# Another placement of the modulation products and five small reorderings in a hand-scheduled fp32 kernel of two transformer blocks

## The reference

```python
for l in range(DEPTH):                                  # DEPTH = 2
    mod_x = (s_x @ w_mod[l] + b_mod[l])[:, None, :]     # (1024) @ (1024, 6144)
    mod_c = s_c @ w_mod[l] + b_mod[l]
    sh1_x, sc1_x, g1_x, sh2_x, sc2_x, g2_x = jnp.split(mod_x, 6, axis=-1)
    h_x = modulate(rms_norm(x, norm_g[l, 0]), sh1_x, sc1_x)
    h_c = modulate(rms_norm(ctx, norm_g[l, 0]), sh1_c, sc1_c)
    m_x, m_c = even_mixer(...) if l == 0 else odd_mixer(...)
    x = x + g1_x * rms_norm(m_x, norm_g[l, 1])
    f_x = squared_relu_mlp(modulate(rms_norm(x, norm_g[l, 2]), sh2_x, sc2_x), w_mlp_in[l], w_mlp_out[l])
    x = x + g2_x * rms_norm(f_x, norm_g[l, 3])
    # the same for ctx in layer 0
```

## Time and profile before

| | us |
|---|---|
| three runs | 1677.31, 1679.67, 1682.97 (median 1679.67) |
| the profiled execution | 1677.31 |
| its span, first to last instruction | 1675.5 |
| mean granted clock of TensorE | 0.968 of full speed |

### The profile page before, as it was taken

How to read it: one execution, slowest core, us unless ns; L and a number is a source line. 1 busy time by engine, 2 the same in 40 slices (tenths; PEclk the granted TensorE clock), 3 DMA queues, 4 the chain that set the end, 5 groups by cost and what they waited for, 6 DMA issues and landing times.

```text
span 1675.5 us, 24174 instructions
## 1 busy us (share of the span) xinstructions
PE 1536.0 (92%) x9546; PEld 1307.6 (78%) x9546; DVE 904.1 (54%) x1513; ACT 677.0 (40%) x1095; POOL 157.7 (9%) x121
## 2 busy tenths in 40 slices
PE   7999899999999568998898999999998988869997
PEld 7998698998987455785688777777787776768886
DVE  6776744544546684436764433333457645555444
ACT  4553444444444324425554222222234534444442
POOL 3100400000000300000014001111002020021110
PEclk9999999999999788999999999999999999979999
DMA  6456555344436123411111543543413510224451
GB/s 247 160 201 227 207 204 201 132 171 140 163 128 229 56 76 151 152 51 51 75 65 62 201 155 147 201 175 140 188 51 110 167 64 1 109 112 176 182 200 52
DMA packets 43338, 233.75 MB, mean 140 GB/s; under 512 B 13088, under 2 KB 14048, under 8 KB 16352
## 3 DMA queue, kind: packets, MB, share of 16 engines
q1 hardware_dynamic: 30944, 222.38, 35.4%
q10 hardware_dynamic: 12288, 9.88, 2.1%
HBM read 231.16 MB, written 1.08 MB: 139 GB/s over the span
## 4 chain that ended last, share of the span: by engine, by line
PE 79%; DVE 11%; ACT 5%; issue 3%; POOL 1%; DMA 1%; ACTq 0%; DVEq 0%; SPq 0%; POOLq 0%
PE ps L516 22%; PE ps L517 21%; PE ps L518 21%; PE ps L719 5%; DVE wlo L979 3%; PE ps L606 2%; PE ps L658 2%; ACT whi L969 2%; PE ps L692 2%; PE ps L650 1%; PE ps L568 1%; POOL flo L2106 1%; DVE nmax L1682 1%; PE ps L590 1%; DVE nmax L1710 1%
## 5 line engine op out<-in xcount | busy, mean ns | idle before, releaser
L979 DVE TENSOR_TENSOR wlo<-raw,whi 128x2048 fp32r<-128x2048 f32 x162 | 383.5, 2393 | 269.3 <-ACT whi L969 269.1
L516 PE MATMUL ps<-fhi,whi 128*128 128x256 f32 (+1 forms) x1280 | 391.3, 306 | 11.7 <-DVE wlo L979 7.2
L969 ACT ACTIVATE whi<-raw 128x2048 fp32r<-128x2048 f32 x162 | 303.8, 1905 | 231.9 <-PE ps L518 177.6
L518 PE MATMUL ps<-fhi,wlo 128*128 128x256 f32 (+1 forms) x1280 | 387.7, 303 | 0.0
L517 PE MATMUL ps<-flo,whi 128*128 128x256 f32 (+1 forms) x1280 | 387.6, 303 | 0.0
L516 PEld LDWEIGHTS ps<-fhi,whi 128*128 128x128 f32 x1280 | 246.4, 192 | 34.5 <-issue 10.3
L518 PEld LDWEIGHTS ps<-fhi,wlo 128*128 128x128 f32 x1280 | 246.3, 192 | 8.9
L517 PEld LDWEIGHTS ps<-flo,whi 128*128 128x128 f32 x1280 | 246.4, 193 | 8.7
L516 PE MATMUL ps<-whi,fhi 128*128 128x512 f32 (+1 forms) x592 | 208.3, 352 | 7.4 <-DVE e_b L1937 3.8
L517 PE MATMUL ps<-wlo,fhi 128*128 128x512 f32 (+1 forms) x592 | 205.2, 347 | 0.0
L518 PE MATMUL ps<-whi,flo 128*128 128x512 f32 (+1 forms) x592 | 205.1, 346 | 0.0
(11 more groups left out here) (220 smaller groups left out, 1823.8 us busy)
## 6 DMA issues: line engine op xcount, KB each, us to landing
raw<-in_wstream SPq DMA_DIRECT2D x210, 1024.0 KB, 4.9
gates<-gated ACTq DMA_DIRECT2D x6, 512.0 KB, 4.5
hx<-in_x SPq DMA_DIRECT2D x1, 1024.0 KB, 5.7
lnrow<-in_ln_g ACTq DMA_DIRECT2D x2, 512.0 KB, 4.2
lnrow<-in_ln_b ACTq DMA_DIRECT2D x2, 512.0 KB, 5.6
hc<-in_ctx ACTq DMA_DIRECT2D x1, 1024.0 KB, 4.8
mix<-in_rpb_rows ACTq DMA_DIRECT2D x4, 256.0 KB, 4.9
hc<-in_rpb_rows ACTq DMA_DIRECT2D x4, 256.0 KB, 3.7
```

What stands on the lines that cost most here:

```text
L516: mm(o, lh, rh, start=start, stop=False)
L518: return mm(o, ll, rh, start=False, stop=stop)
L969: nc.scalar.activation(whi[:, w % SPLIT_SLOTS, :], raw[:, c % RAW_SLOTS, :], ACT.Copy).then_inc(*did("scalar", ("hi", w)))
L979: nc.vector.tensor_tensor(wlo[:, w % SPLIT_SLOTS, :], raw[:, c % RAW_SLOTS, :], whi[:, w % SPLIT_SLOTS, :].bitcast(F32), ALU.subtract).the ...
```

## The change

It has five parts, and all 210 chunks are still loaded and all products made once.

1. The table of the mods. Three now stand early (before `u2`, `u3` and `grp3` of the pooled mixer), one instead of two before the first unit of the dilated attention, four instead of six beside the dilated attention, four instead of five in the part-0 attention, and those of layer 1 come one place earlier in the MLP of layer 0.
2. In the attention of pairs the chunks of `out2,0,1` are split at step 5 on both engines; before, ACT did it at step 12 and DVE after the last item.
3. At the start of layer 0's MLP, the transposes of the normed `x` (`turn_normed(0, 1, 0)`) come after the whole pass g=1 of `in 1`; before, they stood in the middle of it.
4. At the end of that MLP one more tile of `mlp_out` comes ahead of `turn_normed(1, 0, 0)`, and `gated_sums` goes from DVE to POOL.
5. In layer 1 the features of `ctx` (`n1,1,1`) are split after the q tiles are staged; before, ahead of them.

```diff
@@ MODS
-    ('k', 0, 0): [(0, 0), (0, 1)],
-    ('side', 0): [(0, 2)], ('side', 1): [(0, 3)], ('side', 2): [],
+    ('u', 2): [(0, 0)],
+    ('u', 3): [(0, 1)],
+    ('grp', 3): [(0, 2)],
+    ('k', 0, 0): [(0, 3)],
+    ('side', 0): [], ('side', 1): [], ('side', 2): [],
-    ('q2', 0, 1): [(0, 8), (0, 9), (0, 10), (0, 11), (1, 0)],
+    ('q2', 0, 1): [(0, 8), (0, 9), (0, 10), (0, 11)],
-    ('in', 0, 2): [(1, 1)], ('out', 0, 1): [(1, 2)],
...
-    ('in', 0, 7): [(1, 11)],
+    ('in', 0, 1): [(1, 0)], ('out', 0, 0): [(1, 1)],
...
+    ('in', 0, 6): [(1, 10)], ('out', 0, 5): [(1, 11)],
@@ side_steps_pairs
-            return [(1, ("v2", 0, 1, 0)), (3, ("v2", 0, 1, 1)), (12, ("weights",))] + ...
+            return [(1, ("v2", 0, 1, 0)), (3, ("v2", 0, 1, 1)), (5, ("weights",))] + ...
@@ tensor
             for g in range(4):
                 c0 = S if g % 2 == 0 else 0
+                mods_before(("u", g))
                 by_feature(UNIT[("u", g)], ("u", g), c0, c0 + S, feat=("pool", g))
                 if g:
                     group(g - 1)
+            mods_before(("grp", 3))
             group(3)
@@ tensor, MLP of layer 0
-                            for e in range(4):
-                                if (g, j, e) == (1, 1, 2):
-                                    turn_normed(0, 1, 0)
-                                by_feature(UNIT["in", 0, j], ..., tiles=[e], first=g == 1, last=g == 0)
+                            if g:
+                                mods_before(("in", 0, j))
+                            by_feature(UNIT["in", 0, j], ..., first=g == 1, last=g == 0)
+                        if g:
+                            turn_normed(0, 1, 0)
...
                     mlp_out(0, 7, (2, 3), ns=(0,), first=False, last=False)
+                    mlp_out(0, 7, (2,), ns=(1,), first=False, last=False)
                     turn_normed(1, 0, 0)
-                    mlp_out(0, 7, (2, 3), ns=(1,), first=False)
+                    mlp_out(0, 7, (3,), ns=(1,), first=False)
@@ vector, attention of pairs and after it
+                        if at == i and step[0] == "weights":
+                            split_to(("out2", 0, 1), 0)
...
-                    split_to(("out2", 0, 1), 0)
                     low_features(("fo", 0, 0), 0)
@@ vector, layer 1 (ACT alike)
-                if l == 1:
-                    split_to(("k2", 1, 0), 0)
-                    modulate(("n1", 1, 1), 1, 0, 1)
                 for part in range(2 - l):
                     for what, tiles in (("q", range(nt)), ("k", range(4))):
                         split_to((what + "2", l, part))
+                        if l == 1 and what == "k":
+                            modulate(("n1", 1, 1), 1, 0, 1)
@@ vector to pool
-                    gated_sums((0, 1))
-                    gated_sums((2, 3))
+            gated_sums((0, 1))
             low_modulated(("n1", 1, 0), 1, 0, 0)
+            gated_sums((2, 3))
             low_modulated(("n1", 1, 1), 1, 0, 1)
```

More of the change, by code:

```diff
@@ L84, in side_steps @@
                 steps += [(what, qr + 1, g, n) for g in range(NG) for n in range(2)]
-                steps += mods if what == "v" else []
+                steps += mods if what == "q" else []
         else:
@@ L437, in side_steps_pairs @@
         def side_steps_pairs():
-            return [(1, ("v2", 0, 1, 0)), (3, ("v2", 0, 1, 1)), (12, ("weights",))] + [(13 + j // 2, ("fo", j)) for j in range(4)]
+            return [(1, ("v2", 0, 1, 0)), (3, ("v2", 0, 1, 1)), (5, ("weights",))] + [(13 + j // 2, ("fo", j)) for j in range(4)]
         def items_second(l, part):
@@ L802, in _ @@
                             ins.then_inc(*did("tensor", *labels))
-            mod(*MODS["k", 0, 0][0])
+            mods_before(("k", 0, 0))
             turn_features("f1", lambda t: hx[:, t, :], (0, 1), [("ln", 0, 0), ("ln", 0, 1)])
-            mod(*MODS["k", 0, 0][1])
             for what in "kq":
@@ L914, in _ @@
                         for j in range(2):
-                            for e in range(4):
-                                if (g, j, e) == (1, 1, 2):
-                                    turn_normed(0, 1, 0)
-                                by_feature(UNIT["in", 0, j], ("in", 0, j, g), g * S, g * S + S, feat=None if j else ("n2", 0, g),
-                                           tiles=[e], first=g == 1, last=g == 0)
+                            if g:
+                                mods_before(("in", 0, j))
+                            by_feature(UNIT["in", 0, j], ("in", 0, j, g), g * S, g * S + S, feat=None if j else ("n2", 0, g),
+                                       first=g == 1, last=g == 0)
+                        if g:
+                            turn_normed(0, 1, 0)
                     for j in range(1, 8):
@@ L922, in _ @@
                             mods_before(("in", 0, j))
+                            if j == 7:
+                                turn_mod()
                             by_feature(UNIT["in", 0, j], ("in", 0, j), 0, 2 * S)
@@ L1624, in mod_row, with mod_rows @@
                 pending.append((l, j))
+            def mod_rows(name):
+                for m in MODS.get(name, []):
+                    mod_row(*m)
             dve.wait_ge(loads["scol"], 16)
@@ L1628, in _ @@
                 split_to(("u", g))
+                mod_rows(("u", g))
                 if g < 2:
@@ L1637, in _ @@
             split_to(("grp", 3))
+            mod_rows(("grp", 3))
             gate_mixed(3)
@@ L1849, in gated_half @@
                     *did("vector", ("read",) + key, ("gated half", l, which, t, n)))
[L1851 to L1856, removed]
-                        m = mix[:, t, n * NW:(n + 1) * NW]
-                        v.tensor_tensor(m, m, gates[:, t // XT, n * NW:(n + 1) * NW], ALU.mult).then_inc(
-                            *did("vector", ("gated half", 0, 1, t, n)))
             def sum_halves(l, which, group):
@@ L2031, in _ @@
                     normed(0, 1, (0, 1))
+                    for m in MODS.get(("in", 0, 1), []):
+                        mod_row(*m)
                     square_hidden(0, 0, 1)
@@ L2118, in low_hidden, with gated_sums @@
                                     ALU.subtract).then_inc(*did("pool", *labels))
+            def gated_sums(tiles):
+                pool.wait_ge(loads["g01"], 32)
+                for n in range(2):
+                    for t in tiles:
+                        pool.wait_ge(*after("sqh", 0, 1, t, n))
+                        m = mix[:, t, n * NW:(n + 1) * NW]
+                        p.tensor_tensor(m, m, gates[:, t // XT, n * NW:(n + 1) * NW], ALU.mult).then_inc(
+                            *did("pool", ("gated half", 0, 1, t, n)))
             def gain_shift(t, *label):
```

8 lines of the change are left out of this document (2 added, 6 removed), and 8 rows, old and new, of the table MODS.

## The result

| | before | after |
|---|---|---|
| median of the runs, us | 1681.32 (4 runs) | 1721.97 (4 runs) |
| ratio | | 1.0245, 95% interval 1.0233 to 1.0257 |
| span of the profiled execution, us | 1675.5 | 1721.1 |
| mean granted clock | 0.968 | 0.955 |

The changed kernel is 2.45% slower, +40.7 us by the medians. The forecast was 1712 (+33.4), in a range of 1697 to 1727. The median before rests on 4 runs here; 20 later runs of the same kernel have 1679.1, and against these the change costs 42.9.

The account below looks back on a forecast made before the run. TensorE, busy 92% of the span, plus its holes was taken to bound the kernel. 18.8 − 10.2 + 6.5 + 13.3 + 5.0 = +33.4 on 1677.31 gave 1710.7, stated as 1712; the 8 in 10 range was 1697 to 1727.

Parts of the forecast that it names:

- The early mods: Pooled mixer: three mods wait for second chunks held back by raw slots, delaying `u2`, `u3` and `grp 3`: +18.8 us.
- I put 1.6 on it: Pooled mixer, mod (0,0): TensorE runs at half clock for a while after the long hole, costing 1.6 us.
- The dilated attention: Two fewer mods beside it save 2.5 us each: -5.0, bounds -9 to -2.
- The splits in the pairs: Attention of pairs: DVE's low and ACT's high splits at step 5 delay the maxima: +6.5, between 4.5 and 8.3.
- The MLP front: Start of layer 0's MLP: landings for mods (1,0), (1,1) and a hole behind the moved transposes delay `out 0`: +13.3.
- so it lands at 881.3: MLP, mod (1,0): its second chunk takes a slot freed at 876.3 and lands at 881.3; pass g=1 starts 3.0 late.
- Layer 1: Start of layer 1: later features of `ctx` end the last k products at 1305.5, not 1300.4: +5.0, bounds 0 to 8.
- The slots are not what is waited for: Rival: the mods' chunks land in time and part 2 is hidden: -7.6, 1672 us, faster; chance 0.03.
- Only the slots count: Rival: parts 2, 4 and 5 are hidden and the transposes' move costs half: +19, 1698 us; chance 0.20.
- More than I count: Rival: longest landings, part 2 at 8.3, POOL and DVE blocking, slow clock after each new hole: +45, 1724; chance 0.14.
- DVE mostly reads PSUM: Layer 1 start: beside POOL's four multiplications the shared port lock adds nothing; at most 5.1 us, inside the slower rival.
- The estimate of 4.4 us for a landing: DMA skill page's figure for one chunk, against 4.6 shortest in the trace; four landings 2.4 shorter would give 1710.

Follow-up runs that it names:

- p9: Kernel before with mods (0,6) and (0,7) moved from the dilated attention's last quarter into the 19 us hole ahead of block 2: 1681.33 us, ratio 1.0015.
- p4: Kernel before with only the extra `mlp_out` tile, `gated_sums` on POOL and the later features of `ctx`: 1684.88 us, ratio 1.0021.
- p1: Kernel before with only the early half of the mod table, three mods in the pooled mixer and none in the dilated attention's first quarters: 1692.73 us, ratio 1.0065.
- p2: Kernel before with only the splits of `out2,0,1` at step 5 of the attention of pairs, on ACT and DVE: 1687.38 us, ratio 1.0040.

## Why the prediction was right, and where its sizes were off

**The early mods, +18.8 against +24.5.** The mechanism is as forecast: the mod stands at 92 to 93, its second chunk lands 5.0 after the split that gives up its slot, `u2` starts at 102.9 (forecast 101.9), and the other two follow with holes of 2.5 and 3.1. The term that failed in size is the clock: "I put 1.6 on it", once. It acts behind each of the three holes, also behind one of 2.5, and behind the longest on the whole second half of the mod; filling the holes gave 6.0 back. The landings were 5.0, 5.1 and 5.7, counted from the end of the split.

**The dilated attention, -5.0 against -7.5.** Inside my bounds. Two mods fewer save 5.0 of work. Seven holes of 0.9 to 1.5, 8.1 together, stood there before and four stand there after, 4.8 together; one of 0.9 is new. p9, with two mods fewer in the last quarter and the other steps where they were, has all seven holes and gains 4.2 there: so the mods are worth 4 to 5, and the rest is holes. That the other steps' places (18 in a quarter and not 19) made them is a reading, not tested. The profiled execution of before is also among its fastest: in runs that leave this stage as it was, it takes up to 3 longer, in most of them 1.5.

**The part-0 attention (-2.5, -2.9) and mod before in 7 (-2.5, -1.8)** are as forecast.

**The splits in the pairs, +6.5 against +8.0.** I took the middle between 4.5 and 8.3. The upper end was right in size, though not in its sum: DVE has nothing to do for 1.8 until ACT's first high split is done, splits for 4.5, and the next maxima stand behind that in its queue; ACT's second high split does lie beside DVE's first low one. The remaining 1.5 arise two items later.

**The MLP front, +13.3 against +19.6.** Of the forecast's steps, the hole behind the transposes (5.3, measured 5.04), the landing for mod (1,1) (5.0, measured 5.0) and the hole at out 0 that doesn't shrink were right. Wrong was "so it lands at 881.3" for mod (1,0): the landing took 7.6 and made a hole of 3.6, of which the forecast had 1.0. This needed no run to see: the median of 5.0 was taken for a load that took 7.6 in the trace of the kernel before. And again the clock, counted once with 1.6: mod (1,0) 1.0, the pass g=1 1.9, g=0 2.0, mod (1,1) 1.0, so 5.9. The two come to 6.9 more than the forecast has, against the 6.3 by which this place is larger. The reason that I gave for the hole behind the transposes (features over POOL) was not what ended it: TensorE was released by ACT's copy at 928.0, while POOL's last low part ran until 929.1.

**Layer 1, +5.0 against +6.1.** Right in kind: the wait of 3.76 for `e_b` is gone, and the k products wait for `flo`. But the forecast has one term, and the path has three: p4 loses 1.5 ahead of q2 and 1.6 at the turns of ctx before the 3.3 at the k products.

```profile
1338.67 0.55 PE L519 MATMUL ps<-whi,fhi 128*128 128x256 f32 x1 [7.95 <-POOL flo L2107]
```

**The rivals.** *The slots are not what is waited for* is ruled out by the first row of the waits and by p1. *Only the slots count* (+19) falls with p2 and p4, each slower by itself. *More than I count* (+45, 1724) named the right thing, slow clock behind each new hole, and the measured 1722 is nearer to it than to the forecast of 1712. Its sizes, too, fit the stages better: 23.3, 8.3, 16 and 8 against 24.5, 8.0, 19.6 and 6.1. That the time lies inside my range is due to the range being wide enough to take this rival in; the sum itself is a quarter too small against the profiled executions, by 12.2 of 45.6.

The blocking of DVE by POOL was dismissed too early. "DVE mostly reads PSUM" beside the multiplications does not hold: beside the second half of `gated_sums`,

```profile
1307.98 5.01 POOL L2128 TENSOR_TENSOR mix<-mix,gates 128x512 f32<-128x512 f32 x4
```

DVE has short instructions on SBUF, and three of them are stretched:

```profile
1309.70 0.82 DVE L1867 TENSOR_TENSOR sumh<-sumh 128x2 f32<-128x2 f32 x1 [1.32 <-ACT htmp L1268]
1310.55 1.22 DVE L1534 TENSOR_SCALAR dev<-sumh 128x2 f32<-128x2 f32 x1
...
1312.00 1.01 DVE L1540 TENSOR_TENSOR newton<-rstd 128x2 f32<-128x2 f32 x1
```

The same three took 0.15, 0.17 and 0.16 before, and each now ends within 0.03 of the end of one of the multiplications (1310.50, 1311.74, 1313.00); p4 has 0.83, 1.22 and 1.01. And it is on the path. From the first of the three to the residual `hc<-mix,rstd,hc` it took 1.37 before and takes 3.74 now. Without the blocking, by these rows, the first tile of the residual could start when the third multiplication ends, at 1311.74, and the second at 1313.00, so that it would be done at about 1314.3; it is done at 1315.9. That is an estimate of 1.6, nearly all of what this place loses. POOL's slower multiplication alone would then be paid for by the 2.5 of work that DVE loses. A run without the blocking was not made. The prediction also names the wrong work for its longest low split of 5.92: it starts at 67.87, while POOL adds up `sum_b` (67.00 to 71.62); beside POOL's work on `hx`, from 197 on, splits took 4.0 to 4.5. The blocking that it reads from them stands.

The estimate of 4.4 us for a landing went into no term. The Trainium skill, "DMA: Bandwidth & Descriptors", section "Anatomy of one DMA", gives that fit for transfers that GpSimd issues. SP issues these chunks, and their shortest landing between 60 and 200 us was 4.6 before and 4.7 after.

## What to carry to other kernels

Where a ring of buffers feeds an engine, count for each user how long it holds its slot and which event of which engine must end before the load behind it can start. A user that holds a slot across other work costs one whole landing at every place where fewer chunks lie ahead than it needs. Price a hole in TensorE with what comes behind it: here 1 to 2.5 us more, each time, if its own work comes next, and nothing if that waits for another engine anyway. Where a load's landing time carries the forecast, look up that very load in the trace before, and what other transfers are issued at the same moment, and don't take the median.

## What the runs showed of the hardware that I had not expected

The clock of TensorE was already down behind holes of 2.5 us (a unit of 13.2 and not 11.6), and transposes that nobody reads kept it up: eight records of a mod took 1.06 behind them and 1.94 without. In a kernel whose mean clock went from 0.968 to 0.987 by them, the time fell by 0.25% only: where the next work waited for POOL or DVE, the fillers raised the clock and gained nothing. One chunk of 1 MB took 7.6 us with 1 MB of gates loaded beside it, in both kernels, against a median of 5.0. And while POOL multiplied, instructions of DVE that take 0.16 took up to 1.22.
